# Three groups of transposed tiles: from TensorE to 32x32 block transposes on VectorE with a round trip through DRAM

## The reference

```python
# first block, layer i: a sparse attention, a convolution and a pooling branch, then
m = rmsnorm(h, norm_mlp_pre[i])
m = jnp.square(jax.nn.relu(jnp.einsum('bsd,df->bsf', m, w_up[i])))      # 1024 -> 4096
m = jnp.einsum('bsf,fd->bsd', m, w_down[i])                             # 4096 -> 1024
h = h + rmsnorm(m, norm_mlp_post[i])
# second block, layer l
h = swiglu(rmsnorm_2(x, ffn1_pre_g[l]), ffn1_w_in[l], ffn1_w_out[l])    # 1024 -> 2 x 2816 -> 1024
x = x + 0.5 * rmsnorm_2(h, ffn1_post_g[l])
# hybrid mixer: a recurrence (oa), retention with 4 heads of 512 columns (ob), a short convolution (oc)
ob = (jax.nn.silu(g) * ret.reshape(Bsz, S, RET_V)) @ w_ret_out
mix = (ga * oa + gb * ob + gc * oc) @ w_out
# and a second swiglu
```

## Time and profile before

| | |
|---|---|
| time, median of 3 runs | 2320.31 us (2320.28 to 2320.72) |
| span of the profiled execution | 2318.0 us |
| PE busy | 2296.8 us (99%), 12124 matmuls |
| DVE busy | 1540.9 us (66%) |
| ACT busy | 1221.5 us (53%) |
| mean granted TensorE clock | 0.999 of full speed |
| moved by DMA | 434.91 MB, mean 188 GB/s, engines 56.4% of the span |

### The profile page before, as it was taken

The page is one execution under the profiler, slowest core; times in us unless marked ns, Lnnn a source line. Parts: engine busy times, 40 slices in busy tenths (PEclk is TensorE's granted clock), DMA queues, the critical chain, the costliest instruction groups (busy, mean ns, idle before and its releaser), DMA issues.

```text
span 2318.0 us, 30390 instructions
## 1 busy us (share of the span) xinstructions
PE 2296.8 (99%) x12124; PEld 1959.9 (85%) x12124; DVE 1540.9 (66%) x2019; ACT 1221.5 (53%) x1788; POOL 79.1 (3%) x134
## 2 busy tenths in 40 slices
PE   8999999999999999999999999999999999999998
PEld 6888888888888888988888888888889888888887
DVE  6867657776566667876575665665678765756664
ACT  6645446464455556755444554554567553445553
POOL 0110000100000000000000000000000000000000
PEclk9999999999999999999999999999999999999999
DMA  8437655456656555645665465565556456554652
GB/s 334 146 119 238 198 171 209 146 170 203 211 163 217 189 172 163 206 162 183 218 199 191 157 217 192 179 221 190 173 164 214 153 183 221 195 193 164 199 193 89
DMA packets 119805, 434.91 MB, mean 188 GB/s; under 512 B 13553, under 2 KB 13809, under 8 KB 119665
## 3 DMA queue, kind: packets, MB, share of 16 engines
q1 hardware_dynamic: 119664, 432.96, 56.4%
HBM read 431.86 MB, written 1.05 MB: 187 GB/s over the span
## 4 chain that ended last, share of the span: by engine, by line
PE 95%; DVE 4%; ACT 1%; issue 0%; POOL 0%; DMA 0%; DVEq 0%; POOLq 0%; ACTq 0%
PE ub L1716 21%; PE ub L1713 11%; PE ub L1684 9%; PE ub L1686 9%; PE ub L1685 9%; PE acc L1684 8%; PE acc L1685 8%; PE acc L1686 8%; PE ub L1691 1%; PE ub L1692 1%; PE ub L1693 1%; PE acc L1747 1%; DVE wlo L1020 1%; DVE work L1208 1%; PE acc L2162 0%; DVE best L1205 0%
## 5 line engine op out<-in xcount | busy, mean ns | idle before, releaser
L1020 DVE TENSOR_TENSOR wlo<-raw,whi 128x1024 fp32r<-128x1024 f32 x776 | 913.1, 1220 | 215.2 <-ACT whi L534 213.4
L534 ACT ACTIVATE whi<-raw 128x1024 fp32r<-128x1024 f32 x776 | 777.3, 1052 | 200.9 <-PE ub L1686 140.5
L1716 PE MATMUL ub<-xhl,whi 128*128 128x512 f32 x2176 | 514.6, 390 | 0.0
L1716 PEld LDWEIGHTS ub<-xhl,whi 128*128 128x128 f32 x2176 | 404.2, 188 | 82.7 <-issue 1.3
L1684 PE MATMUL acc<-whi,bhl 128*128 128x512 f32 x736 | 288.2, 392 | 0.0
L1685 PE MATMUL acc<-wlo,bhl 128*128 128x512 f32 x736 | 286.6, 389 | 0.0
L1686 PE MATMUL acc<-whi,bhl 128*128 128x512 f32 x736 | 286.5, 389 | 0.0
L1684 PE MATMUL ub<-whi,xhl 128*128 128x512 f32 (+1 forms) x704 | 275.3, 391 | 3.0 <-DVE wlo L1020 1.5
L1713 PEld LDWEIGHTS ub<-xhl,wlo 128*128 128x128 f32 x2176 | 272.0, 191 | 6.2
L1713 PE MATMUL ub<-xhl,wlo 128*128 128x256 f32 x2176 | 275.4, 283 | 0.0
L1686 PE MATMUL ub<-whi,xhl 128*128 128x512 f32 (+1 forms) x704 | 272.5, 387 | 0.0
(11 more groups left out here) (305 smaller groups left out, 2471.7 us busy)
## 6 DMA issues: line engine op xcount, KB each, us to landing
raw<-in_w SPq DMA_DIRECT2D x776, 512.0 KB, 5.0
gain<-in_gains SPq DMA_DIRECT2D x20, 512.0 KB, 7.8
tapw<-in_taps SPq DMA_DIRECT2D x16, 512.0 KB, 4.3
DEC<-in_decay SPq DMA_DIRECT2D x2, 768.0 KB, 8.1
par<-in_par SPq DMA_DIRECT2D x2, 647.0 KB, 9.4
par<-in_par SPq DMA_DIRECT2D x2, 556.0 KB, 7.2
H<-in_x SPq DMA_DIRECT2D x2, 512.0 KB, 4.5
out_h<-H SPq DMA_DIRECT2D x4, 256.0 KB, 2.6
```

The lines of the kernel that those rows point to most:

```text
L534: do(act.activation(whi[:, s % RING, c], raw[:, slot, c], ACT.Copy), counts["w_hi"])
L1020: do(dve.tensor_tensor(wlo[:, s % RING, c], raw[:, PLACES[s][0], c], whi[:, s % RING, c].bitcast(f32), ALU.subtract), counts["w_lo"])
L1716: last = pe.matmul(bank, whi[:, s % RING, n:n + P], xhl[:, kt, :, :].rearrange("p a n -> p (a n)"), start=first, stop=stop, skip_group_che ...
```

## The change

Three kinds of tiles are no longer transposed by PE: those of `turn_first`, of `turn_p` and of `turn_m(0)`. In their place:

1. DVE transposes each 128x512 tile in blocks of 32x32 (`to_blocks`, one `dve.transpose` a tile) into a buffer `FB` or `PB` in SBUF.
2. SP writes the buffer to a scratch tensor in DRAM (`put`, one DMA) and reads it back (`get`, four DMAs) in such a way that the blocks lie where a full transpose would have them. A group is 1 MB in the first block's feed-forward, 512 KB elsewhere.
3. ACT (`moved`, which waits for the four reads) and DVE make `bhi` and `blo` from SBUF in place of PSUM.

```diff
 def ffn1_order():
-    seq = [("first", j) for j in range(4)] + [("up", 4), ("up", 5), ("up", 6)]
-    for j in range(9):
-        seq += [("down", j), ("up", j + 7)]
-    return seq + [("down", j) for j in range(9, 16)]
+    seq = [("first", j) for j in range(4)] + [("up", j) for j in range(4, 9)]
+    for j in range(7):
+        seq += [("down", j), ("up", j + 9)]
+    return seq + [("down", j) for j in range(7, 16)]
...
         FH = sb("FH", 0, at=unit(48), shape=[P, 4, 512])
+        FB = sb("FB", 0, at=unit(56), shape=[P, 2048])
...
+        PB = sb("PB", 0, at=unit(16), shape=[P, RET_HEADS, 1024])
...
+        def in_blocks(t, k, n):
+            return t.rearrange("p (c n q i) -> p c n q i", c=4, n=n, q=4)[:, :, k, :, :].rearrange("p c q i -> p q c i")
+        def moved_blocks(t, k, n):
+            return t.rearrange("p (a n q i) -> p a n q i", a=4, n=n, q=4)[:, :, k, :, :].rearrange("p a q i -> p q a i")
...
+                def put(event, src):
+                    done[event] += 1
+                    sp.wait_ge(sem[event], done[event])
+                    g = done["put"]
+                    done["put"] += 1
+                    sp.dma_start(turned_rows[g * P:(g + 1) * P, 0:src.shape[1]], src).then_inc(sem["put"], 16)
+                def get(dst):
+                    g = done["get"]
+                    done["get"] += 1
+                    sp.wait_ge(sem["put"], 16 * (g + 1))
+                    n = dst.shape[1] // 4
+                    for c in range(4):
+                        sp.dma_start(dst[32 * c:32 * c + 32, :].rearrange("j (a x) -> j a x", a=4),
+                                     turned_rows[g * P:(g + 1) * P, c * n:(c + 1) * n].rearrange("(a j) x -> j a x", a=4)
+                                     ).then_inc(sem[f"moved{g % 2}"], 16)
...
                         if s == s1(L, "ffn", 10):
+                            put("blocked", FB[:, :])
+                        if s == s1(L, "ffn", 12):
+                            get(FB[:, :])
+                        if s == s1(L, "ffn", 10):
                             sp.wait_ge(sem["xn_ready"], 8 * L + 8)
                             load_gain(1, 4 * L + 4)
...
+                        for name in ("f1", "f2"):
+                            if s == s2(L, name + "first", 10):
+                                put("blocked", FB[:, 0:1024])
+                            if s == s2(L, name + "first", 12):
+                                get(FB[:, 0:1024])
+                        for hd in range(RET_HEADS):
+                            if s == s2(L, "g", 0) + 2 * hd + 7:
+                                put("pb", PB[:, hd, :])
+                            if s == s2(L, "g", 0) + 2 * hd + 8:
+                                get(PB[:, hd, :])
+                        if s == s2(L, "sco", 1) + 8:
+                            put("blocked", FB[:, 0:1024])
+                        if s == s2(L, "sco", 1) + 9:
+                            get(FB[:, 0:1024])
...
+                def moved():
+                    nxt(f"moved{arrivals[0] % 2}", 64)
+                    arrivals[0] += 1
+                def first_hi(blocks_):
+                    moved()
+                    for t in range(2):
+                        for b in range(blocks_):
+                            do(act.activation(by_blocks(bhi[:, 4 * b:4 * b + 4, cols(t)]),
+                                              moved_blocks(FB[:, 0:1024 * blocks_], 2 * b + t, 2 * blocks_), ACT.Copy),
+                               counts["hh"])
...
-                            if j == 4:
-                                first_hi(((0, 1), (1, 1)))
+                            if j == 6:
+                                first_hi(2)
...
                                 squares_o(hd)
+                                if hd >= 2:
+                                    turned_p(hd - 2)
...
+                            if j in (0, 2):
+                                turned_p(2 + j // 2)
...
+                def to_blocks(dst, k, n, source, count=None):
+                    return do(dve.transpose(in_blocks(dst, k, n), source.rearrange("p (q c i) -> p q c i", c=4, i=32)), count)
...
+                        settle()
+                        for t in range(2):
+                            to_blocks(PB[:, hd, :], t, 2, tX[:, t, :], counts["pb"] if t else None)
...
+                        if (kind, j) in (("g", 6), ("ya", 0), ("ya", 1), ("ya", 3)):
+                            turned_p(dict(g=0, ya=1)[kind] + (j + 1) // 2 * (kind == "ya"))
...
-                    def turn_first(b, t):
...
-                    def turn_p(hd):
...
                     if event == "pd":
-                        return max(j + 1, 5)
-                    return max(2 * j, 3)
+                        return max(j + 1, 7)
+                    return max(2 * j, 5)
...
-                            if (kind, j) == ("gc", 3):
-                                turn_m(0)
```

More of the change, by code:

```diff
@@ L306, in s2 @@
         def s2(L, name, j=0):
+            if name in ("f1first", "f2first"):
+                return LAYERS * B1["end"] + L * B2["end"] + AT2[name, 0] + j
             return LAYERS * B1["end"] + L * B2["end"] + AT2[name, j]
@@ L576, in sines_by_token @@
                     do(act.activation(cc[:, :, 8:16], yc, ACT.Sin), counts["sin_ready"])
-                def first_hi(pieces):
-                    for b, t in pieces:
-                        nxt("tr_done")
-                        do(act.activation(bhi[:, 4 * b:4 * b + 4, cols(t)], quad(acc[:, 2 * b + t, :]), ACT.Copy),
-                           counts["hh"])
+                arrivals = [0]
+                def moved():
[8 more added lines that the diff above has]
+                               counts["hh"])
                 act.wait_ge(sem["x_in0"], 16)
@@ L920, in _ @@
                         nxt("va_done")
-                        do(act.activation(Vhi[:, 0, fcol(vb)], ub[:, 2 * vb, :], ACT.Copy), counts["vah"])
+                        do(act.activation(Vhi[:, vb, 0, :], ub[:, 2 * vb, :], ACT.Copy), counts["vah"])
                     for vb in range(2):
@@ L983, in _ @@
                             blocks_ += 1
-                            if (kind, j) == ("gc", 3):
-                                turned_m(0)
+                        elif (kind, j) == ("sco", 2):
+                            turned_m(0)
                         elif kind == "sc":
@@ L1029, in gain_in, with rest_of, first_lo, first_blocks @@
                     dve.wait_ge(sem[f"g_in{slot}"], 16 * gains_seen[slot])
-                def first_lo(pieces):
-                    for b, t in pieces:
-                        nxt("hh")
-                        do(dve.tensor_tensor(blo[:, 4 * b:4 * b + 4, cols(t)], quad(acc[:, 2 * b + t, :]),
-                                             bhi[:, 4 * b:4 * b + 4, cols(t)].bitcast(f32), ALU.subtract),
-                           counts["hid"])
+                def rest_of(t, u, source):
+                    return dve.tensor_tensor(by_blocks(blo[:, u:u + 4, cols(t)]), source,
+                                             by_blocks(bhi[:, u:u + 4, cols(t)].bitcast(f32)), ALU.subtract)
+                def first_lo(blocks_):
+                    for t in range(2):
+                        for b in range(blocks_):
+                            nxt("hh")
+                            do(rest_of(t, 4 * b, moved_blocks(FB[:, 0:1024 * blocks_], 2 * b + t, 2 * blocks_)),
+                               counts["hid"])
+                def to_blocks(dst, k, n, source, count=None):
+                    return do(dve.transpose(in_blocks(dst, k, n), source.rearrange("p (q c i) -> p q c i", c=4, i=32)), count)
+                def first_blocks(t, blocks_):
+                    settle()
+                    for b in range(blocks_):
+                        to_blocks(FB[:, 0:1024 * blocks_], 2 * b + t, 2 * blocks_, FH[:, 2 * b + t, :],
+                                  counts["blocked"] if t and b == blocks_ - 1 else None)
                 def post(t, bank):
@@ L1521, in weighed @@
                                    counts["mixed"] if final and t else None)
+                        if final and f == 0:
+                            settle()
+                            for t in range(2):
+                                to_blocks(FB[:, 0:1024], t, 2, MIX[:, t, 0:512], counts["blocked"] if t else None)
                     norms(ffn("f1"))
@@ L1612, in _ @@
                             weighed(j // 2, final=kind == "sco")
-                        elif (kind, j) == ("gc", 3):
+                        elif (kind, j) == ("sco", 2):
                             turned_m(0)
@@ L1797, in take @@
                             fill(U_[2 * b + t], "fp")
-                    def turn_first(b, t):
-                        pe.wait_ge(sem["fp"], fp0 + (t if gated else 2 * t + b) + 1)
-                        A_[2 * b + t].take(pe, sem["hid"], hid0 + (2 * t + 1 if gated else 3 * t + b + 1))
```

(15 more changed lines are left out.)

92 lines of the change are left out of this document (41 added, 51 removed).

## The result

The changed kernel takes 2343.49 us (median of 4 runs, 2341.10 to 2344.13), the kernel before 2320.38: ratio 1.0098, 95% interval 1.0084 to 1.0112. It is slower by 1%; the forecast was 2317, range 2306 to 2324. The profiled execution has a span of 2341.6 us, 23.6 more than before, at a mean granted clock of 0.993.

A forecast was written before the change was run, and what follows sets the result against it. PE was taken to bound the kernel, with 95% of the chain of waits. Span 2318.0 - 16.0 (saved starts) + 11.2 (waits at down 0) + 1.6 (ya) = 2314.8, plus 2.3 to the median: 2317 us, range 2306 to 2324.

The forecast's parts named there:

- What PE saves: On PE, 144 transposes go, priced by distance of starts: 16.0 us saved, bounds 14.0 and 16.8.
- DVE's transposes: 36 tiles of 128x512 on DVE at 0.7 us each, in feed-forwards hidden in its idle time at no cost.
- The ya steps: PE waits 0.75 us for a bank at gb 0, 1.6 us in two layers; bounds 0.3 to 4.2.
- The new wait: First block's feed-forward: down 0 waits 5.6 us for the reads, 11.2 in two layers; bounds 4 to 16.
- the other 2.6 at 0.335 to 0.355 MB/us: First block's feed-forward: the queue's last 2.6 MB move at that rate after 185.1 and are through at 192.7.
- So the reads land at 194.3: First block's feed-forward, layer 0: reads land 194.3, bytes through at 192.7, a landing some 1.7 us after its bytes.
- 2318.0 - 16.0 + 11.2 + 1.6: Whole kernel: old span, less PE's saved starts, plus down 0's waits and the ya waits, giving 2314.8 us of span.
- The other groups hide: Round trips in the second block's feed-forwards, retention and the mix are covered and cost nothing.
- 2.7 us in hand: Mix: remainders ready 19.2 us after sco 1, mix 0 starts at 21.9, so no wait.
- Rival 2: Reads in 1 and 2 KB pieces run at a third of the speed, wait 11.8 us a layer; 2330, chance 0.13.
- Rivals 1, 3 and 4: 1: reads in time, 2307, 0.24; 3: freed starts given back, 2320 to 2321, 0.09; 4: transpose costs its duration, 2293.5, 0.04.

The follow-up runs named there:

- the kernel without waits: Against the changed kernel: copies and downs moved later in both feed-forwards, the mixed sum's write and reads one weight chunk sooner; 2304.62 us, ratio 0.9932.
- retention alone: Changed kernel with the change kept only in retention, PE transposing the other tiles again; 2314.58 us, ratio 0.9976 against the kernel before.
- the first block alone: Changed kernel with the change kept only in the first block's feed-forward, PE transposing the other tiles again; 2342.84 us, ratio 1.0097 against the kernel before.

## Why the prediction was wrong, by its own steps

The span came out 26.8 us above the forecast 2314.8. By the prediction's terms: the wait at down 0 5.2 more; matmuls at the low clock and what goes with the waits, 12.3, for which it had no term; the groups that were to hide 11.2 (second block 6.2, mixed sum 5.0); the ya steps 0.9 and other idle time 1.0 less. The first alone would have given 2322, inside the range; the other two, both put at nothing, carried the time out of it.

- **What PE saves: right as a sum.** 16.0 forecast, 16.0 measured between before and the kernel without waits. By place errors cancel: PE's busy time falls by 3.6 for the first block (forecast 3.6), 5.8 for retention (7.1), 3.9 for the second block (3.5) and 2.7 for the mixed sum (1.8). The duration of 272 ns would have given 39.6; the distance of starts was the price.
- **DVE's transposes: right.** 0.70 us, hidden where it was said. That retention alone gave -5.6 where -5.5 was forecast is in part luck: 5.8 of PE's busy time against 7.1, and 0.8 of waits against 1.6.
- **The ya steps: right in kind, half the size.** 0.4 a layer, forecast 0.75.
- **The new wait: right in kind, but "the other 2.6 at 0.335 to 0.355 MB/us", "So the reads land at 194.3" failed.** They landed at 198.0. The order of the queue, SP's times and PE's arrival were right. The rate was taken from a stretch of weight loads, which land in 128 partitions; reads that land in 32 halve the rate of the whole queue. Waits of 9.6 and 6.8 against 5.6 each, 16.4 where the bound for both was 16. The prediction did say that no row shows such pieces, and bounded the transfers at 243 GB/s; the 213 of the changed kernel and the 153 to 216 of the first block alone lie below that. A bound from the slowest row at hand is no bound for a shape that no row has.
- **The sum "2318.0 - 16.0 + 11.2 + 1.6": a term was missing, and it is the largest.** PE's busy time fell by 3.7, not by 16.0. Of the 12.3 us between them 9.6 can be read from the distance of starts, against that at the full clock: 4.9 behind down 0's two waits (starts 0.43 apart for 4.0 us in layer 0 and for 6.1 in layer 1), 1.7 behind the mixed sum's wait in layer 0, and 1.5 each behind two of the second block's. The other 2.7 I can't place. The earlier trace rows never show a PE that stands idle for long, so nothing in the sum spoke of it.
- **"The other groups hide": wrong in two places.** Second block: the wait for the reads was compared with when down 0 needs them. But ACT stands in it from behind up 6 on, and up 7's result, which it has not copied, keeps the bank that up 9 needs: PE waits 2.6, 1.7 and 1.9 in three of the four. For the first block the prediction asked what stands behind ACT's wait; for the second it did not. Mixed sum: in place of "2.7 us in hand" mix 0 waited 0.5. The remainders were done 22.4 us after sco 1, forecast 19.2, as SP issued the write 2.6 us after its data were ready, behind waiting weight loads. And PE's second half waits for a sum that stands behind the remainders in DVE's list, and that was not looked at.
- **Rivals.** Rival 2 had the sign, and with 11.8 us a layer and 2330 it came nearest, 13 us short; its mechanism, pieces of 2 KB, is wrong, since whole 8 KB rows ran no faster, and the 32 partitions of the same reads were the cause. Rivals 1, 3 and 4 are refuted: the reads were late, and the freed starts are all there.

The ledger of the 23.6 us of span: -16.0 starts, +27.3 idle, +12.3 busy, most of it at the low clock. Open are the 2.7 us above and why waits of much the same length end with the low clock or without it. A read that lands in 64 partitions was not tried.

## What to carry to other kernels

A round trip through DRAM costs nothing where nobody stands in front of it, and then every start taken from the engine that bounds is won. For each wait that an edit adds to an engine that works in order, ask three things: what stands behind it, whose buffers that holds, and what else in the same list, such as a store that a waiting load holds up, keeps it from being met sooner. Let reads land across all partitions, with a large outermost dimension (32 and 128 kept all engines busy here, 4 did not), and do the shuffling in the write. And count a wait on PE as more than its length: here five waits of 1.9 to 9.6 us cost 1.5 to 3 us more each in slower matmuls, two of 1.7 and 2.3 next to nothing.

## What the runs showed of the hardware

- While reads of 1 MB as four DMAs that land in 32 partitions each are under way, the queue moves 153 to 225 GB/s with the engines full (windows of 2 us from 190 to 196 us), for 2 KB and 8 KB pieces alike, from the scratch and from the weights. With the reads over 128 partitions: 406 to 430. With writes that leave from 32 partitions: 353 to 376.
- By the mean of all packets, the weight packets in the same queue were slowed as well (0.27 us for 3.4 KB, where 4 KB took 0.16).
- A read with an outermost dimension of 4 kept the work of four of 16 engines busy (0.26, 102 GB/s).
- PE idle since 191.6: granted clock 0.99 up to 195 us, then 0.50, with starts 0.43 us apart until it rose, some 4 us after work began again. Waits of 1.9, 2.3 and 2.6 us were followed by windows of 5 us at 0.69, 0.66 and 0.66, one of 1.7 and another of 2.3 by windows at 1.00.
- DVE transposed a 128x512 fp32 tile in 32x32 blocks in 0.70 us.
